# Even mixer of a two-block network on one core: sigmoid ahead of silu, gated scores one slot earlier, output units reordered

## What is computed

```python
def even_mixer(u, w_in, w_out, lb, onorm_g, sinks, cos_b, sin_b):
    qa, fa, ia, ga, qb, kb, vb = jnp.split(u @ w_in, EVEN_SPLITS, axis=-1)
    oa = hgrn2_chunkwise(qa, fa, ia, lb)                # gated part, 4 heads
    oa = rmsnorm(oa, onorm_g) * jax.nn.silu(ga)
    ob = swa_with_sinks(apply_rope(qb), apply_rope(kb), vb, sinks)   # window attention, 8 heads
    return jnp.concatenate([oa, ob], axis=-1) @ w_out

def hgrn2_chunkwise(q, f_logit, i, lb):                 # chunks of 64 rows
    qf = jax.nn.silu(q)
    f = lb + (1.0 - lb) * jax.nn.sigmoid(f_logit)
    k = 1.0 - f
    b = jnp.cumsum(jnp.log(f))
    q_s, k_s, k_d = qf * jnp.exp(b), k * jnp.exp(-b), k * jnp.exp(b_last - b)
    # masked q_s k_s^T times v inside a chunk, and a decayed state from chunk to chunk
```

## Time and profile before

| what | value |
|---|---|
| median of three runs | 1446.65 us (1446.36 to 1446.94) |
| the profiled execution, its own time | 1447.43 us |
| span of its first to last instruction | 1445.4 us |
| PE, matmuls | 1415.1 us busy, 98% |
| DVE | 871.6 us, 60% |
| ACT | 714.1 us, 49% |
| POOL | 77.1 us, 5% |
| share of the chain of waits that ended last: PE, DVE, ACT, DMA | 84%, 7%, 4%, 3% |

### The profile page before, as it was taken

One profiled execution on the slowest core, in us unless ns is written; L12 is line 12 of the kernel. 1 busy time (PEld: TensorE's weight loads), 2 busy tenths in 40 slices (PEclk: granted clock), 3 DMA queues, 4 the chain that ended last, 5 costly groups with the idle time before them and its releaser, 6 DMA issues.

```text
span 1445.4 us, 17117 instructions
## 1 busy us (share of the span) xinstructions
PE 1415.1 (98%) x6598; PEld 1169.9 (81%) x6598; DVE 871.6 (60%) x811; ACT 714.1 (49%) x726; POOL 77.1 (5%) x91
## 2 busy tenths in 40 slices
PE   7999999999999999999999999999999999999997
PEld 6888887878888887878888878888888878888886
DVE  6869686775463666764644574644674545654536
ACT  4674766545343557653543453443443445453434
POOL 0000000010000200110000110000202101100001
PEclk9999999999999999999999999999999999999999
DMA  9747544465454453445554565555453533654541
GB/s 394 290 152 260 186 162 172 159 226 216 179 207 171 175 211 117 146 166 198 192 189 183 193 225 182 207 185 187 177 209 141 206 144 122 242 179 169 195 184 44
DMA packets 40380, 272.51 MB, mean 189 GB/s; under 512 B 4609, under 2 KB 5505, under 8 KB 8706
## 3 DMA queue, kind: packets, MB, share of 16 engines
q1 hardware_dynamic: 36864, 261.65, 49.6%
q10 hardware_dynamic: 3458, 10.04, 2.0%
HBM read 270.62 MB, written 1.05 MB: 188 GB/s over the span
## 4 chain that ended last, share of the span: by engine, by line
PE 84%; DVE 7%; ACT 4%; DMA 3%; issue 2%; POOL 0%; SPq 0%; ACTq 0%; DVEq 0%; POOLq 0%
PE acc L2061 26%; PE acc L2063 26%; PE acc L2062 26%; PE turn L2114 3%; DVE wlo L1189 3%; DMA raw<-in_units 2%; ACT whi L420 1%; DMA mod_raw<-in_units 1%; DVE h L1259 1%; DVE xn L1243 0%; PE aux L2598 0%; PE turn L2263 0%; DVE feed_lo L1227 0%; DMA gpost<-in_g_final 0%; DVE xn L1252 0%
## 5 line engine op out<-in xcount | busy, mean ns | idle before, releaser
L1189 DVE TENSOR_TENSOR wlo<-raw,whi 128x2048 fp32r<-128x2048 f32 x233 | 533.1, 2298 | 263.0 <-ACT whi L420 262.9
L2061 PE MATMUL acc<-whi,feed_hi 128*128 128x512 f32 (+1 forms) x1496 | 595.7, 398 | 5.5 <-DVE wlo L1189 4.5
L2063 PE MATMUL acc<-whi,feed_lo 128*128 128x512 f32 (+1 forms) x1496 | 583.6, 390 | 0.0
L2062 PE MATMUL acc<-wlo,feed_hi 128*128 128x512 f32 (+1 forms) x1496 | 582.8, 390 | 0.0
L420 ACT ACTIVATE whi<-raw 128x2048 fp32r<-128x2048 f32 x233 | 445.3, 1916 | 256.5 <-PE acc L2063 241.1
L2061 PEld LDWEIGHTS acc<-whi,feed_hi 128*128 128x128 f32 x1496 | 282.2, 189 | 66.1 <-DVE wlo L1189 6.7
L2063 PEld LDWEIGHTS acc<-whi,feed_lo 128*128 128x128 f32 x1496 | 281.9, 188 | 59.9
L2062 PEld LDWEIGHTS acc<-wlo,feed_hi 128*128 128x128 f32 x1496 | 282.3, 189 | 56.1 <-issue 1.2
L2061 PE MATMUL acc<-whi,hid_hi 128*128 128x512 f32 x352 | 138.0, 392 | 0.0
L2063 PE MATMUL acc<-whi,hid_lo 128*128 128x512 f32 x352 | 137.1, 389 | 0.0
L2062 PE MATMUL acc<-wlo,hid_hi 128*128 128x512 f32 x352 | 137.0, 389 | 0.0
(11 more groups left out here) (326 smaller groups left out, 859.5 us busy)
## 6 DMA issues: line engine op xcount, KB each, us to landing
raw<-in_units SPq DMA_DIRECT2D x237, 1024.0 KB, 4.9
mod_raw<-in_units SPq DMA_DIRECT2D x6, 1024.0 KB, 10.7
gpost<-in_norm_g ACTq DMA_DIRECT2D x8, 512.0 KB, 4.9
gpre<-in_norm_g ACTq DMA_DIRECT2D x6, 512.0 KB, 6.1
mod_more<-in_units SPq DMA_DIRECT2D x2, 1024.0 KB, 23.3
h<-in_x SPq DMA_DIRECT2D x2, 512.0 KB, 10.1
w_ax<-in_w_ax SPq DMA_DIRECT2D x1, 1024.0 KB, 26.5
bgate<-in_b_gate SPq DMA_DIRECT2D x1, 1024.0 KB, 27.8
```

Source lines behind the costliest of these rows:

```text
L1189: dve.tensor_tensor(wlo[:, u % RING, :], raw[:, u % RING, :], whi[:, u % RING, :].bitcast(F32), ALU.subtract).then_inc(lo_ready, 1)
L2061: pe.matmul(out, xh, wh, start=first, stop=False)
L2062: pe.matmul(out, xh, wl, start=False, stop=False)
L2063: return pe.matmul(out, xl, wh, start=False, stop=last)
```

## The change

On ACT the sigmoid (with the wait for the forget gate's turns) and the logarithm, with `probs_turned(2)` between them, come ahead of the query's silu. On PE `hgrn_scores` goes from slot 26 to slot 25, `hgrn_mix` from 27 to 26, `hgrn_fed` from 29 and 31 to 28 and 30, and the order of the output units becomes: attention half of tile 0 (26, 27), first attention unit of tile 1 (28), gated half of tile 0 (29, 30), second attention unit of tile 1 (31), gated half of tile 1 (32, 33). On ACT and DVE the `hi`, `lo` and `fed` calls behind the scores are put in another order. Nothing is added or removed.

```diff
 # ACT
-                for name in ("g0", "g1"):
-                    received(name)
-                act.activation(qsT[:, :, :], qsT[:, :, :], ACT.Silu).then_inc(q_silu, 1)
                 for name in ("f0", "f1"):
                     received(name)
                 act.activation(fT[:, :, :], fT[:, :, :], ACT.Sigmoid).then_inc(f_sig, 1)
...
                 for a in range(A_HEADS):
                     act.activation(ff[:, a, :], fT[:, a, :], ACT.Ln, scale=om_lb[:, a:a + 1],
                                    bias=lb[:, a:a + 1]).then_inc(logs_ready, 1)
+                for name in ("g0", "g1"):
+                    received(name)
+                act.activation(qsT[:, :, :], qsT[:, :, :], ACT.Silu).then_inc(q_silu, 1)
                 values(0)
...
                 sums(1, units=1)
                 act.activation(pp[1][:, 1, :], acc[1][:, :], ACT.Copy).then_inc(acc_free[1], 1)
-                hi()
-                fed("s1", 4, 1)
                 for t in range(TOK):
                     mix()
                     act.activation(xn[:, t, 0:BANK], aux[:, t, :], ACT.Square).then_inc(sq_ready, 1)
+                hi()
+                fed("s1", 4, 1)
                 fed("h0", 0, 0)
-                hi(2)
+                hi()
                 fed("h1", 0, 1)
 
                 sums(0)
                 square_sum(acc[0][:, :], xn[:, 0, :])
+                hi()
                 feed(feed_hi, 0)
 # DVE, behind the four masked copies
-                lo()
-                fed("s1", 4, 1)
                 for t in range(TOK):
                     dve.wait_ge(sq_ready, t + 1)
...
                     ins.then_inc(hgrn_out, 1)
+                fed("s1", 4, 1)
+                lo()
                 fed("h0", 0, 0)
-                lo(2)
+                lo()
                 fed("h1", 0, 1)
...
                 feed(feed_lo, feed_hi, 0)
-                lo()
+                lo(2)
                 sums(1, U_EVEN_OUT)
 # PE
-                slots += [("out_swa", 13 + k, k, t) for t in range(TOK) for k in range(2)]
-                slots += [("out_hgrn", 15 + k, k, t) for t in range(TOK) for k in range(2)]
+                swa, hgrn = ([[(kind, at + k, k, t) for k in range(2)] for t in range(TOK)]
+                             for kind, at in (("out_swa", 13), ("out_hgrn", 15)))
+                slots += swa[0] + swa[1][0:1] + hgrn[0] + swa[1][1:2] + hgrn[1]
...
                     if s == 25:
                         swa_fed(0)
+                        hgrn_scores()
                     if s == 26:
-                        hgrn_scores()
+                        hgrn_mix()
                     if s == 27:
                         swa_fed(1)
-                        hgrn_mix()
-                    if s in (29, 31):
-                        hgrn_fed(0 if s == 29 else 1)
+                    if s in (28, 30):
+                        hgrn_fed(0 if s == 28 else 1)
```

## The result

The changed kernel took 1451.88 us in the median of 8 runs (1451.02 to 1452.23), the kernel before beside it 1447.59 us in 8 runs (1446.36 to 1448.92): ratio 1.0029, 95% interval 1.002 to 1.0037. It is slower, by 4.3 us. The forecast was 1448.8 with a range up to 1450.7, and the time lies above it. A second set on another occasion gave 1450.97 against 1447.37 us, ratio 1.0026 (1.0016 to 1.0036).

What follows compares the result with a forecast made beforehand. The prediction took PE as the bound, busy for 1415.1 of 1445.4 us. It added +0.5 us without the clock and +1.7 for the clock, +2.2 in sum, to the median 1446.65: 1448.8 us, range 1446.1 to 1450.7.

Steps and rivals of the forecast that it cites:

- the clock: Behind PE's wait in the scores: the granted clock falls once, +1.7 us, bounds 0 and 3.4.
- long half clock: Rival: behind the scores' wait the clock stays low for two stretches instead of one, 3.4 us; chance 0.17.
- the walk: Step-by-step sum over the mixer and the units behind it, without the clock: +0.5 us, bounds -0.6 and +1.5.
- Sigmoid ahead of silu: ACT and PE's mix: the wait at 570.17 goes; of 1.17 us, 0.52 is left as gain.
- the rival: A fifth table load on ACT, silu between logarithm and exponential: 1.3 us more, 1450.1 us; chance 0.06.
- Scores one slot up: PE at head 2 of the gated scores: stands still 3.8 us for DVE's first masked copy.
- The units reordered: PE's output units behind the scores: waits of 1.36 and 0.73 us for the next norm's rows vanish.
- One thing is late next: DVE's two `lo` ahead of scaling the second tile: tile 1's chain and the `lo` behind it 0.5 us later.
- The sum without the clock: All steps up to the fourth unit of the next part: +0.5 us, bounds -0.6 and +1.5.

Runs made afterwards that it cites:

- slot_behind: Changed kernel with the first masked copy's wait ahead of slot 25 and heads 2 and 3 behind that slot: ratio 1.0029, again 1.0025.
- copies_old_order: copies_first with the old order of the output units and the gated rows turned ahead of slots 29 and 31: 1446.88 us, ratio 1.0.
- copies_first: Changed kernel with DVE's four masked copies behind one subtraction, ahead of the split of s0 and two more subtractions: 1444.98 us, ratio 0.9985.
- fill: Changed kernel with 15 more 512-column matmuls on PE ahead of head 2's wait, their result overwritten: 1448.59 us, ratio 1.0008.
- scores_back: Changed kernel with the gated scores back at slot 26 and the mix at slot 27: 1448.40 us, ratio 1.001.
- act_only: Kernel before with only ACT's order changed, sigmoid and logarithm ahead of the query's silu: 1448.33 us, ratio 1.0011.
- copies_silu_back: copies_first with the query's silu ahead of the sigmoid again on ACT: 1445.29 us, ratio 0.9981.
- act_fill: act_only with 4 more 512-column matmuls on PE ahead of head 2's wait: 1446.90 us, ratio 0.9995.
- order_back: Changed kernel with the old order of the output units and gated rows turned ahead of slots 29 and 31: 1455.36 us, ratio 1.0052.
- copies_again: The kernel of copies_first run once more, with nothing else changed: 1443.98 us, ratio 0.9974.

## Why the prediction was wrong

**The term that failed** is the clock: "I take the fall, once: +1.7 us". I had priced it by the one fall in the trace of before: 3.80 us with a granted clock of 0.55, 0.45 x 3.80 = 1.7; at 0.50 that is 3.4 us long. I took one because the new stretch, with PE busy for 0.6 of 4.40 us by my estimate, was idler than the one ahead of that fall (1.45 of 4.40), and where 2.30 of 4.40 were busy it had stayed at 1.00. The profile showed 6.8 us at 0.50 (3.4 us) and in another execution 10.2 us (4.8 us), the second outside the term's own bounds of 0 and 3.4. My long half clock, two such stretches behind the wait in place of one, named place and price (3.4) rightly, and its distance of +3.9 is what the first profile gave to 0.1 us; I gave it 0.17 for want of a row that showed a longer fall. Its reason, the 64-column matmuls behind the wait, isn't shown: with 512-column matmuls there (slot_behind) the clock was low for 6.8 us too. What the traces show is 1.00 ahead of the wait and 0.50 behind it.

**The range** missed for a second reason. I added the difference to the median of three runs, 1446.65, while more runs put the kernel before at 1447.1 to 1447.8. With the long fall the forecast would have been 1446.65 + 3.9 = 1450.6, still 1.3 below the measured time; with 1447.6 it is 1451.5. The range should have had the spread of before's clock falls in it. It also took the long fall only with the walk's middle, +0.5; with the walk's own upper bound of +1.5 it would have ended at 1446.65 + 4.9 = 1451.5. And of the walk's bounds, -0.6 and +1.5, only the upper one has the half microsecond of rounding.

**What held**, by the steps:
- *Sigmoid ahead of silu:* PE's wait at the mix went from 1.0 to 0.5 us and to 576.84; ACT's stretch stayed in place. The table loads stayed five, each 1.28 us (before at 564.92, 567.29, 570.42, 577.52 and 589.74, after at 564.58, 567.71, 571.10, 577.19 and 589.41), now with the silu between logarithm and exponential; the one more that the rival priced at 1.3 us didn't come.
- *Scores one slot up:* forecast 3.8 us of standing still from start to start, measured 3.8 (589.53 to 593.30, the last start before it at 589.34 and 0.2 for it), listed as a wait of 3.58.
- *The units reordered:* no wait above 0.2 us at the rows, the eight turns in one go (625.25); worth 2.0 us (copies_old_order against copies_first), of the 2.1 us of waits.
- *One thing is late next:* the wait for the last subtraction was to be about 0.8, is 0.57 as listed, from 0.28.
- *The sum without the clock:* +0.5 forecast, +0.65 measured (fill), and +0.5 in the first profile less its 3.4 us of clock.

The time moved up, as the forecast had it. But the prediction gave 0.68 to staying within 0.2% and 0.26 to more than that upward, and the measured move is 0.29%.

## What to carry to other kernels

Moving work on PE one slot earlier helped here only when the engine that hands it its next operand came earlier too: PE ran into a wait, since DVE's queue was left as it was, and moving three calls in DVE's queue turned the loss of 4 us into a gain of 2 to 4. Price a new idle stretch of PE not by its length alone but with the clock behind it, 1.7 to 4.8 us where it fell here, and read that price from as many falls as can be found. Where a kernel's runs spread by more than the effect, compare the distance between two instructions around the change as well as the times.

## What the runs showed of the hardware

The low clock lasted 3.4, 6.8 or 10.2 us, and nothing between, in every fall of the 14 profiles between 20 and 1400 us (9, 8 and 2 falls, the granted clock 0.50 in each). It doesn't need a long wait: behind 0.8 us of waiting among short matmuls it fell in two of two profiles (scores_back, act_only), behind 0.3 us in the profile of the kernel before it did not (1.00). Nor does every wait bring it: behind the 1.0 us at the mix of heads 2 (before, copies_silu_back) it didn't fall (1.00 from 565 to 580), and behind the two waits for the next norm's rows it fell in three of five profiles (act_fill, copies_old_order, order_back; not in before and act_only).

Whether it falls differs between executions of one program, and with it the time. copies_first and copies_again are the same kernel, and their distances agree to 0.03 us. At the next change of stage, which none of these kernels touches, the windows from 840 to 870 us differ in the granted clock. Here are the kernel before, copies_first and copies_again, with 0.94, 0.89 and 1.00:

```profile
840.00:870.00 30.00, 27.05 (x116) 21.65 (x115) 19.89 (x18) 15.98 (x17) 4.14 (x5) 0.94 0.71 261
```

```profile
840.00:870.00 30.00, 26.68 (x110) 21.21 (x110) 17.42 (x15) 14.28 (x13) 3.26 (x5) 0.89 0.68 247
```

```profile
840.00:870.00 30.00, 27.21 (x127) 21.92 (x126) 17.62 (x15) 14.20 (x14) 2.77 (x3) 1.00 0.75 267
```

That is 1.8, 3.3 and 0 us lost. The spans of the two executions of the same kernel are 1443.6 and 1440.3 us. The kernel before spreads from 1444.88 to 1449.98 us over all its runs, which falls like these (up to 4.8 us each) would explain, an estimate. What decides in the single execution wasn't tried and stays open.
